# A two-layer diffusion backbone on one core: another spread of the modulation products over the feed-forward blocks, and side matmuls dealt out in thirds inside an attention step

## The reference

```python
for l in range(2):
    mod  = silu(c)     @ w_mod[l] + b_mod[l]    # six vectors of 1024 (shift, scale, gate, twice)
    modc = silu(c_ctx) @ w_mod[l] + b_mod[l]    # the same for the context tokens
    h  = rms_norm(x,  g1) * (1 + sc1)  + sh1
    hc = rms_norm(xc, g1) * (1 + scc1) + shc1
    p, pc = h @ w_in, hc @ w_in
    # three mixers: chunked mLSTM, latent attention (mla, 8 heads), neighbourhood attention (na, 8 heads)
    y = (g_a * (ml @ Wa) + g_b * (mla @ Wb) + g_c * (na @ Wc)) @ w_out   # g_* = sigmoid of columns of p
    x = x + gate1 * y
    x = x + gate2 * (relu(norm(x) @ w_ff1) ** 2 @ w_ff2)
```

## Time and profile before

| | |
|---|---|
| time, median of 3 | 2029.62 us (2029.49 to 2030.04) |
| the profiled execution | 2029.49 us, its span 2027.7 us |
| mean granted TensorE clock | 0.916 of full speed |
| PE busy, share of span | 84% |
| DVE, ACT, POOL busy | 52%, 36%, 30% |
| feed-forward part of layer 0 | about 897 to 1256 us of the span |
| attention phases | about 386 to 510, 630 to 759, 1508 to 1585, 1674 to 1752 us |

### The profile page before, as it was taken

How to read it: one execution, slowest core, us unless ns; L and a number is a source line. 1 busy time by engine, 2 the same in 40 slices (tenths; PEclk the granted TensorE clock), 3 DMA queues, 4 the chain that set the end, 5 groups by cost and what they waited for, 6 DMA issues and landing times.

```text
span 2027.7 us, 24668 instructions
## 1 busy us (share of the span) xinstructions
PE 1706.7 (84%) x9538; PEld 1445.4 (71%) x9538; DVE 1062.0 (52%) x1891; ACT 731.0 (36%) x1382; POOL 612.8 (30%) x364
## 2 busy tenths in 40 slices
PE   3595668999858999889999998767699859888998
PEld 1383548877646778758888786756688648788998
DVE  6796962234055333435866666336236274556555
ACT  3213333344243442343323132333335344435443
POOL 0341113322211212134545453421422311234443
PEclk8797779999868999999999999779799879999999
DMA  6452212211110113213344535210312202344553
GB/s 249 159 192 83 83 48 89 66 60 53 60 32 32 54 57 116 95 61 126 144 172 160 196 136 221 91 68 1 94 63 84 91 16 94 136 160 145 185 187 125
DMA packets 55847, 216.99 MB, mean 107 GB/s; under 512 B 17313, under 2 KB 17459, under 8 KB 41139
## 3 DMA queue, kind: packets, MB, share of 16 engines
q1 hardware_dynamic: 41232, 202.13, 28.3%
q10 hardware_dynamic: 14499, 13.29, 2.1%
HBM read 210.15 MB, written 5.24 MB: 106 GB/s over the span
## 4 chain that ended last, share of the span: by engine, by line
PE 69%; DVE 16%; ACT 5%; issue 3%; POOL 3%; DMA 2%; ACTq 1%; POOLq 0%; DVEq 0%; SPq 0%
PE bank L1532 36%; PE bank L1574 9%; PE bank L1546 6%; PE bank L1807 3%; PE bank L1694 3%; PE bank L1786 3%; DVE mjunk L1025 3%; PE bank L1556 3%; DVE acc L1025 2%; ACT wH L654 2%; PE bank L1793 2%; DVE arena L1168 1%; POOL wL L524 1%; POOL wL L526 1%; DVE wL L1010 1%
## 5 line engine op out<-in xcount | busy, mean ns | idle before, releaser
L654 ACT ACTIVATE wH<-raw 128x1280 fp32r<-128x1280 f32 (+5 forms) x380 | 295.4, 833 | 623.6 <-PE bank L1532 430.8
L526 POOL TENSOR_TENSOR wL<-raw,wH 128x768 fp32r<-128x768 f32 (+5 forms) x190 | 329.1, 1736 | 474.1 <-ACT wH L654 474.1
L524 POOL TENSOR_TENSOR wL<-raw,wH 128x1280 fp32r<-128x1280 f32 (+5 forms) x98 | 231.2, 2359 | 647.3 <-ACT wH L654 647.3
L1532 PE MATMUL bank<-hH,wH 128*128 128x512 f32 (+1 forms) x976 | 345.5, 354 | 81.4 <-DVE hL L1062 36.8
L1532 PE MATMUL bank<-hL,wH 128*128 128x512 f32 (+1 forms) x976 | 339.6, 348 | 0.0
L1532 PE MATMUL bank<-hH,wL 128*128 128x512 f32 (+1 forms) x976 | 339.4, 348 | 0.0
L1532 PEld LDWEIGHTS bank<-hH,wH 128*128 128x128 f32 x976 | 192.0, 197 | 113.9 <-issue 55.1
L1532 PEld LDWEIGHTS bank<-hL,wH 128*128 128x128 f32 x976 | 192.5, 197 | 20.9 <-issue 0.5
L1532 PEld LDWEIGHTS bank<-hH,wL 128*128 128x128 f32 x976 | 191.8, 197 | 21.6
L1532 PE MATMUL bank<-oH,wH 128*128 128x512 f32 (+1 forms) x576 | 195.2, 339 | 4.2 <-POOL wL L526 4.2
L1010 DVE TENSOR_TENSOR wL<-raw,wH 128x1280 fp32r<-128x1280 f32 (+1 forms) x92 | 121.3, 1326 | 141.8 <-ACT wH L654 141.4
(11 more groups left out here) (205 smaller groups left out, 3118.0 us busy)
## 6 DMA issues: line engine op xcount, KB each, us to landing
raw<-in_p_ff SPq DMA_DIRECT2D x64, 1024.0 KB, 4.8
acc<-in_p_mod SPq DMA_DIRECT2D x48, 1024.0 KB, 5.2
raw<-in_p_ml SPq DMA_DIRECT2D x12, 1024.0 KB, 7.1
raw<-in_p_na SPq DMA_DIRECT2D x12, 1024.0 KB, 4.8
raw<-in_p_mga SPq DMA_DIRECT2D x16, 512.0 KB, 3.5
raw<-in_p_mgc SPq DMA_DIRECT2D x16, 512.0 KB, 3.5
raw<-in_p_mgb SPq DMA_DIRECT2D x8, 1024.0 KB, 4.8
raw<-in_p_out SPq DMA_DIRECT2D x8, 1024.0 KB, 4.8
```

What stands on the lines that cost most here:

```text
L524: pool.tensor_tensor(l_[:, 0:cut], r_[:, 0:cut], h_[:, 0:cut].bitcast(F32), ALU.subtract)
L526: pool.tensor_tensor(l_[:, cut:k * w], r_[:, cut:k * w], h_[:, cut:k * w].bitcast(F32), ALU.subtract)\
L654: act.activation(flat(wH, n)[:, part], flat(raw, n)[:, part], ACT.Copy)\
L1532: ins = pe.matmul(dst, w_[:, kk, c:c + P], r_[:, kk, lo:TOK], start=kk == k0 and m == 0, stop=kk == k0 + kn - 1 and m == 2)
```

## The change

There are two independent edits. First, the mods of layer 1 are spread six to a group, on the blocks j = 1, 4, 5, 5, 6, 7. Their loads stand directly behind the load of the block with the same number, not of the block after. On DVE a mod now comes after `share_ahead` and after the second `hidden_low` of its block. Second, the side matmuls of a step are taken in three equal portions: behind S, behind T and behind O (3, 3, 3 in layer 0 and 6, 6, 6 in layer 1), where all of them stood behind O.

```diff
-def ff_mods(j):
-    i, q = j // 8, j % 8 - 4
-    if j < 0 or q < 0:
-        return ()
-    return (MODS + 4 * i + q,) if i < 2 else (MODS + 8 * (i - 1) + 2 * q, MODS + 8 * (i - 1) + 2 * q + 1)
+FF_MODS = [[MODS + 6 * (j // 8) + q for q in ((), (0,), (), (), (1,), (2, 3), (4,), (5,))[j % 8]] for j in range(32)]
...
                         load(n)
                         if (name, l) == ("ff", 0):
-                            for m in ff_mods(j - 1):
+                            for m in FF_MODS[j]:
                                 load_mod(m)
-                    if (name, l) == ("ff", 0):
-                        for m in ff_mods(31):
-                            load_mod(m)
...
                             residual(u, 2 * (j - 4), M_GATE2)
-                        if l == 0:
-                            for m in ff_mods(8 * i + j):
-                                mod(m)
                         share_ahead(n0 + 8 * i + j)
                         if j < 3:
                             hidden_low(u, i, j, 1)
+                        if l == 0:
+                            for m in FF_MODS[8 * i + j]:
+                                mod(m)
...
                             pe.matmul(bank[4 + step % 2][:, 0:nk], q_, k_, start=True, stop=True).then_inc(S(tag + "s").up(1), 1)
+                            pump(pace // 3)
...
                             ins.then_inc(S(tag + "pt").up(1), 1)
+                        if step < len(items):
+                            pump(pace // 3)
...
                             ins.then_inc(S(tag + "o").up(1), 1)
                         if step < len(items):
-                            pump(pace)
+                            pump(pace - 2 * (pace // 3))
```

## The result

The changed kernel takes 2088.97 us (median of 4 runs, 2088.91 to 2089.32) where the kernel before takes 2029.55 us in the same comparison (4 runs, 2029.15 to 2030.04). The ratio is 1.0293 with a 95% interval of 1.0275 to 1.0310: 59.4 us slower. The prediction was slower by 39.5 us, at most 53.5, so its direction was right and 2089 us lies above its range. The profiled execution of the changed kernel took 2091.81 us with a span of 2090.1 us.

The account below looks back on a forecast made before the run. PE was taken to bound the kernel for about seven tenths of the span. Mods +27.5 and side matmuls +12.1 made +39.6 us on 2029.49, so 2069 us; forecast 2060 to 2078 (0.60), range 2042 to 2083.

Parts of the forecast that it names:

- The four late blocks: Layer 0 feed-forward: one late block per group makes PE wait 9.25, 9.25, 6.95 and 5.2 us, 30.65 in sum.
- the train that was written out: Layer 0 feed-forward: residual, mod, SP issue, landing, then split before PE starts, 20.15 us from the end of block 4.
- The slow stretches: Layer 0 feed-forward: each of four gaps brings PE matmuls at the lower clock, 2.6 us more each, 10.4 in all.
- What comes back: Layer 0 feed-forward: the gap at block 23 goes, 6.8 us, and the layer's end to the norm shortens by 6.8.
- The side matmuls in layer 0: Layer 0 attention: 5.6 us added for changes of kind, 2.6 us of O's waits saved.
- changes of kind: Layer 0 attention: PE switching to side matmuls behind T costs 0.09 us in each of 62 steps, 5.6 us.
- Layer 0 nets +3.0: Layer 0 attention: the second edit's added and saved time there come to 3.0 us slower.
- The side matmuls in layer 1: Layer 1 attention: moved side matmuls lengthen the loop by 0.7 us per two steps, 9.1 us over thirteen periods.
- six side matmuls stand between: Layer 1 attention: six side matmuls between T and O add 0.8 us to the loop, 0.1 taken back.
- Behind S no cost is taken: Attention: a portion behind S priced at nothing; at the same cost, 96 steps would add 8.6 us.
- The upper end for the second edit: Attention of both layers: the side matmuls' new order costs at most +21 us.
- Rival 3: Feed-forward and attention: more late blocks, longer slow stretches and a cost behind S, about 2084 us; chance 0.10.

Follow-up runs that it names:

- the experiment: First edit alone (mods respread, loads on the same block), all side matmuls behind O as in the kernel before: 2060.31 us, ratio 1.0144.
- e6: Kernel before with, in layer 1 only, six side matmuls of a step behind S and twelve behind O: 2049.77 us, ratio 1.0096.
- e7: Kernel before with side matmuls in thirds in both layers and layer 1's gate tanh one ACT step earlier: 2047.23 us, ratio 1.0086.
- e11: Kernel before with layer 1's side matmuls in thirds, but no gate or branch block beginning ahead of T or O: 2031.42 us, ratio 1.0006.
- e5: Kernel before with, in layer 1 only, six side matmuls of a step behind T and twelve behind O: 2042.58 us, ratio 1.0071.
- e3: Changed kernel's mod spread with each mod's load one block later, attention as in the kernel before: 2029.80 us, ratio 0.9999.
- e4: Kernel before with the side matmuls in thirds in layer 0's attention only: 2034.28 us, ratio 1.0022.

## Why the prediction was right, and where it failed

- **The four late blocks: right.** They are at blocks 6, 14, 22 and 30, by the train that was written out. Gaps: 9.9, 10.0, 7.5 and 5.8 us, 33.2 in all, where 30.65 was predicted. The 2.5 more come from POOL's first subtraction, 3.6 to 3.7 us against 2.92. Landings were 6.90 to 7.17 (7.15 taken). One slip changed nothing: in group 3 the mod waited for is 43, not "45"; both have two sums.
- **The slow stretches: right in kind.** 336 matmuls took 78.4, 78.3 and 79.3 us where 0.227 each makes 76.3, and the 48 behind the last gap 12.8 for 10.9: 2.1, 2.0, 3.0 and 1.9, together 9.0 for 10.4.
- **What comes back: right.** No gap at block 23 (6.8), and 6.9 us for 13.4 at the end of the layer. The first edit sums to 33.2 + 9.0 - 6.8 - 6.5 = +28.9 us by these; the trace shows +29.4, the experiment +30.9, the prediction said +27.5.
- **The side matmuls in layer 0: one term wrong, the sum near by luck.** The waits of O for L1406 are gone, 2.6 us, as predicted. The 5.6 us for changes of kind do not show: the phases are 0.4 us shorter each, with a new wait of 0.8 us at the end of each. What the trace has is 2.8 us behind the phase, from the clock, which the prediction did not have. "Layer 0 nets +3.0" came near by chance.
- **The side matmuls in layer 1: the step that failed.** The prediction made "9.1 us" of it: "six side matmuls stand between: 6 x 0.12 + 0.09 = 0.8 us in the loop", of which it took 0.7, and "Behind S no cost is taken". It measured 27.2 us (13.3 + 13.9). The first of these terms was about right: behind T, six matmuls add 0.71 us less the 0.09 that O comes out shorter. The second is the one that failed. The portion behind S adds 1.6 us to a period that grew by 2.2: PE waits 0.85 us longer, for the PSUM bank that the tanh frees, and then runs 0.95 us of side matmuls, less 0.22 that T comes out shorter. The prediction asked how long the moved matmuls run and what a change of kind costs, and never what the first one waits for. Behind O the wait for the bank cost nothing, since by then the tanh was done. Behind S it is met while ACT is still at the exponential. PE's chain shows T and O behind the side matmuls, so they are late too. e6, with the portion behind S alone, shows 1.49 us a period, the 1.6 less the 0.09 at O; taking away the cause of this wait (e7) gives 13.4 us back; and with no portion between T and O, and none ahead of the T that is in the loop (e11), nothing measurable is left of the loss.
- **The bounds.** The upper end for the second edit, 21, stood on more changes of kind. A bound on a wait is not found in a row of a running time; the row to ask for was when the releaser of the moved instruction's wait ends. Rival 3 (2084) came nearest in size, and named a cost behind S, but no wait that would make one.

## What to carry to other kernels

When work is moved ahead of an instruction that a loop waits for, ask two things: what the moved work waits for, and whether the place is in the loop. A wait that was free in the old place is paid in full in the new one, with everything behind it; work that waits for nothing still costs its running time there (e5). Put it into the step in which nobody waits for the engine (e11). When loads are respread over a queue, ask of each one that waits whose finish it waits for, what is written behind it, and how far ahead of its use that must land; a load that waits for the step just before it makes the next block late by the whole train. Evening out an uneven schedule pays only at the places that were late: here the double mods of two groups, 0.8% with the rest left alone.

## What the runs showed of the hardware

- A gap of 2.7 us on TensorE was followed by the lower granted clock: the next matmuls came 0.43 us apart where they had come 0.23 apart (e3). The 288 matmuls behind it took 67.15 us where 0.227 each makes 65.4, so the slow stretch added 1.8 us to a gap of 2.7.
- The clock also fell at a phase's end at which PE's two last pauses, 1.27 and 1.46 us, were as long as before; only the stretch ahead of them had thinned, from 4.93 to 3.87 us of work in 5 (e4). Side work behind the last instruction of a phase is worth something for that alone; I had not looked there.
- GpSimd's subtraction takes 2.92 us when it starts beside nothing, and 3.1 to 3.7 when it is issued into a running VectorE sum: 3.09 with 0.21 us of the sum left (e3), 3.74 with 0.93 left. A sum issued behind it takes 3.9 in place of 1.2.
